# The down product of a mixture-of-experts layer: one full-precision product, or three products of rounded and remaining parts

## The reference, cut to what matters

```python
def hier_moe(h, p):
    ...
    hg = jnp.einsum('nd,edf->nef', x, p['moe_w_gate'])
    hu = jnp.einsum('nd,edf->nef', x, p['moe_w_up'])
    act = jax.nn.silu(hg) * hu * combine.astype(x.dtype)[..., None]
    y = jnp.einsum('nef,efd->nd', act, p['moe_w_down'])
    return y.reshape(b, t, d)
```

## Time and profile before

| | |
|---|---|
| median of 3 runs | 1420.52 us (1415.59 to 1420.88) |
| profiled execution: its own time as listed, the span from first to last instruction | 1411.4 us |
| TensorE busy | 1236.9 us, 88% of the span |
| VectorE busy | 678.2 us, 48% |
| ScalarE busy | 491.7 us, 35% |
| read from HBM | 295.61 MB, 211 GB/s over the span |

### The profile page before, as it was taken

How to read it: one execution, slowest core, us unless ns; L and a number is a source line. 1 busy time by engine, 2 the same in 40 slices (tenths; PEclk the granted TensorE clock), 3 DMA queues, 4 the chain that set the end, 5 groups by cost and what they waited for, 6 DMA issues and landing times.

```text
span 1411.4 us, 18228 instructions
## 1 busy us (share of the span) xinstructions
PE 1236.9 (88%) x7508; PEld 968.0 (69%) x7508; DVE 678.2 (48%) x857; ACT 491.7 (35%) x550; POOL 86.5 (6%) x93
## 2 busy tenths in 40 slices
PE   4689678998679999999967996798886999999997
PEld 3489568797656666666664985687776666666665
DVE  0255535443355556656423654445424556566652
ACT  2234521112244444444213444111322544444440
POOL 0000203130000000000000011222100000000000
PEclk8799879999789999999988997899996999999999
DMA  9744600121508888888865354102060488888960
GB/s 389 337 179 179 242 9 31 35 90 44 225 0 336 338 338 339 346 345 336 343 269 244 146 199 172 34 31 94 1 243 26 179 345 335 335 340 344 354 268 32
DMA packets 15195, 299.00 MB, mean 212 GB/s; under 512 B 1920, under 2 KB 1920, under 8 KB 2176
## 3 DMA queue, kind: packets, MB, share of 16 engines
q1 hardware_dynamic: 14688, 296.67, 53.5%
q0 software_dynamic: 416, 1.05, 0.2%
HBM read 295.61 MB, written 2.10 MB: 211 GB/s over the span
## 4 chain that ended last, share of the span: by engine, by line
PE 79%; DVE 6%; issue 5%; ACT 5%; DMA 3%; POOL 1%; SPq 0%; DVEq 0%; POOLq 0%; ACTq 0%
PE ps L824 16%; PE ps L795 8%; PE ps L796 8%; PE ps L797 8%; PE ps L713 4%; PE ps L483 3%; PE ps L485 3%; PE ps L484 3%; PE ps L663 3%; PE ps L638 3%; PE ps L659 3%; DMA param<-in_param 3%; PE ps L459 2%; PE ps L838 1%; PE ps L862 1%
## 5 line engine op out<-in xcount | busy, mean ns | idle before, releaser
L1602 DVE TENSOR_TENSOR ring_r<-ring,arena_r 128x2048 fp32r<-128x2048 f32 x124 | 284.3, 2292 | 129.5 <-ACT arena_r L1127 129.5
L1127 ACT ACTIVATE arena_r<-ring 128x2048 fp32r<-128x2048 f32 x124 | 236.7, 1909 | 231.2 <-PE ps L797 231.2
L795 PE MATMUL ps<-arena_r 128*128 128x512 f32 x512 | 231.3, 452 | 5.4 <-DVE ring_r L1602 3.5
L824 PE MATMUL ps<-ring,arena 128*128 128x512 f32 x512 | 230.3, 592 | 1.0 <-DVE arena L1608 1.0
L797 PE MATMUL ps<-ring_r,arena_r 128*128 128x512 f32 x512 | 202.5, 395 | 0.0
L796 PE MATMUL ps<-arena_r 128*128 128x512 f32 x512 | 202.3, 395 | 0.0
L824 PEld LDWEIGHTS ps<-ring,arena 128*128 128x128 f32 x512 | 96.8, 189 | 99.0 <-issue 91.9
L795 PEld LDWEIGHTS ps<-arena_r 128*128 128x128 f32 x512 | 96.3, 188 | 38.9 <-issue 16.7
L483 PE MATMUL ps<-arena_r 128*128 128x256 f32 x384 | 109.7, 286 | 10.4 <-DVE ring_r L1256 10.4
L796 PEld LDWEIGHTS ps<-arena_r 128*128 128x128 f32 x512 | 96.6, 189 | 31.8 <-issue 14.4
L797 PEld LDWEIGHTS ps<-ring_r,arena_r 128*128 128x128 f32 x512 | 96.0, 188 | 22.6
(11 more groups left out here) (301 smaller groups left out, 1548.9 us busy)
## 6 DMA issues: line engine op xcount, KB each, us to landing
ring<-in_moe SPq DMA_DIRECT2D x64, 3072.0 KB, 10.1
ring<-in_ada_w SPq DMA_DIRECT2D x16, 3072.0 KB, 11.1
ring<-in_w_feat SPq DMA_DIRECT2D x8, 3072.0 KB, 14.1
ring<-in_w_tok SPq DMA_DIRECT2D x2, 2112.0 KB, 24.0
ring<-in_w_out SPq DMA_DIRECT2D x2, 2048.0 KB, 7.3
ring<-in_w_out SPq DMA_DIRECT2D x4, 1024.0 KB, 4.9
param<-in_param SPq DMA_DIRECT2D x2, 1501.5 KB, 23.4
const<-in_const SPq DMA_DIRECT2D x1, 1899.0 KB, 16.6
```

The source lines that it names most:

```text
L795: mm(out, x_hi, hi[:, k], start=k == 0, stop=False)
L824: done = mm(bank(4 + half), act_t[:, i % 2, kk * P:(kk + 1) * P], ring[i % RING][:, at:at + 512], start=i == 0 and kk == 0, stop=i == PER_ ...
L1127: go(w_hi[:, 0:4096].rearrange("p (w n) -> p w n", w=2)[:, :, cols], ring[j][:, 0:4096].rearrange("p (w n) -> p w n", w=2)[:, :, cols], AC ...
L1602: tt(low_w, raw_w, high_w, ALU.subtract).then_inc(sem[name], 1)
```

## The change

The down product is computed like gate and up. ScalarE rounds the down weights of one expert into `down_hi` (one buffer, in a part of `param` that is free by then; 2048 columns), VectorE subtracts that from the ring slot in place. The transposed activations are rounded by ScalarE into `act_h` instead of being copied by VectorE, and VectorE subtracts to get `act_l`. TensorE makes twelve fp32r products in place of four full-precision ones. ScalarE's rounding of the down weights of e + 1 waits for the down product of e, as there is one `down_hi`. Some semaphores get the names that the other branch uses, and increments that kept unused ones in step fall away. The diff, cut to its core:

```diff
 # buffers
-        g_silu, gat, act_t = (halves(arena[:, after_w + n * 512:after_w + (n + 1) * 512]) for n in range(3))
+        g_silu, gat = (halves(arena[:, after_w + n * 512:after_w + (n + 1) * 512]) for n in range(2))
+        act_h, act_l = (halves(arena_r[:, at:at + 512]) for at in (after_w + 1024, 8192))
+        down_hi = param_r[:, PARAM["ck"].start:PARAM["ck"].start + 2048]
...
 # TensorE
                     if i >= 0:
-                        pe.wait_ge(sem["act_t"], rise(l, "act_t", e + 1))
+                        pe.wait_ge(sem["act_lo"], rise(l, "act_lo", e + 1))
+                        pe.wait_ge(sem["lo_down"], rise(l, "lo_down", e + 1))
                         if i == 0:
                             pe.wait_ge(sem["yg_lo"], rise(l, "yg_lo", turn + 1))
                         for half in range(2):
                             for kk in range(2):
-                                at = 4096 + kk * D_MODEL + half * 512
-                                done = mm(bank(4 + half), act_t[:, i % 2, kk * P:(kk + 1) * P], ring[i % RING][:, at:at + 512],
-                                          start=i == 0 and kk == 0, stop=i == PER_GROUP - 1 and kk == 1, skip_group_check=True)
+                                at = kk * D_MODEL + half * 512
+                                hi, lo = down_hi[:, at:at + 512], ring_r[i % RING][:, 4096 + at:4096 + at + 512]
+                                x_hi, x_lo = (x[:, i % 2, kk * P:(kk + 1) * P] for x in (act_h, act_l))
+                                mm(bank(4 + half), x_hi, hi, start=i == 0 and kk == 0, stop=False, skip_group_check=True)
+                                mm(bank(4 + half), x_lo, hi, start=False, stop=False, skip_group_check=True)
+                                done = mm(bank(4 + half), x_hi, lo, start=False, stop=i == PER_GROUP - 1 and kk == 1, skip_group_check=True)
                         done.then_inc(sem["down_mm"], 1)
...
 # ScalarE
+                def high_down(e, j):
+
+                    go(down_hi, ring[j][:, 4096:SLOT], ACT.Copy).then_inc(sem["hi_down"], 1)
+
                 def gathered_step(e, i, turn, ahead=2):
 
+                    if i >= 0:
+                        act.wait_ge(sem["tr_mm"], rise(l, "tr_mm", e + 1))
+                        go(act_h[:, i % 2], bank(2 + i % 2, FF), ACT.Copy).then_inc(sem["act_hi"], 1)
                     if ahead > 1:
-                        high_half(e + 2, (i + 2) % RING, "hi_a", "half_mm", 0)
+                        high_half(e + 2, (i + 2) % RING, "hi_a", "gate_mm", 0)
...
                     if ahead > 1:
-                        high_half(e + 2, (i + 2) % RING, "hi_b", "gu_mm", 1)
+                        high_half(e + 2, (i + 2) % RING, "hi_b", "up_mm", 1)
+                    if ahead > 0:
+                        if i >= 0:
+                            act.wait_ge(sem["down_mm"], rise(l, "down_mm", e + 1))
+                        high_down(e + 1, (i + 1) % RING)
...
 # VectorE
                     if i >= 0:
-                        dve.wait_ge(sem["tr_mm"], rise(l, "tr_mm", e + 1))
-                        copy(act_t[:, i % 2], bank(2 + i % 2, FF)).then_inc(sem["act_t"], 1)
+                        dve.wait_ge(sem["act_hi"], rise(l, "act_hi", e + 1))
+                        tt(act_l[:, i % 2], bank(2 + i % 2, FF), act_h[:, i % 2], ALU.subtract).then_inc(sem["act_lo"], 1)
...
                     if ahead > 1:
                         low_half(e + 2, (i + 2) % RING, "lo_b", "hi_b", 1)
+                    if ahead > 0:
+                        dve.wait_ge(sem["hi_down"], rise(l, "hi_down", e + 2))
+                        j = (i + 1) % RING
+                        tt(ring_r[j][:, 4096:SLOT], ring[j][:, 4096:SLOT], down_hi, ALU.subtract).then_inc(sem["lo_down"], 1)
```

More of the change, by code:

```diff
@@ L140 @@
     ht_hi=4, ht_lo=4, sel=1, ga_mm=8, ga_hi=8, ga_lo=8, cg_mm=1, cg_dve=1, st_mm=2, st_act=2,
-    half_mm=32, gu_mm=32, tr_mm=32, hi_a=31, hi_b=31, lo_a=31, lo_b=31, g_silu=32, g_act=32, act_t=32, yg_hi=4, yg_lo=5,
+    tr_mm=32, hi_a=31, hi_b=31, lo_a=31, lo_b=31, yg_hi=4, yg_lo=5,
     scatter_mm=4,
@@ L797, in gate_up @@
                         last = mm(out, x_hi, lo[:, k], start=False, stop=k == KT - 1)
-                    last.then_inc(sem["half_mm" if first_half else "gu_mm"], 1)
+                    last.then_inc(sem["gate_mm" if first_half else "up_mm"], 1)
                 def gathered_step(e, i, turn, last=False):
@@ L808, in gathered_step @@
                     if i >= 0:
-                        pe.wait_ge(sem["g_act"], rise(l, "g_act", e + 1))
+                        pe.wait_ge(sem["prod"], rise(l, "prod", e + 1))
                         for kk in range(2):
@@ L865, in _ @@
                             last.then_inc(sem["scatter_mm"], 1)
-                    for name, n in (("cb_mm", 16), ("gate_mm", 32), ("up_mm", 32)):
-                        pe.sem_inc(sem[name], n)
+                    pe.sem_inc(sem["cb_mm"], 16)
                 with pe.Else():
@@ L897, in _ @@
                         step(e, e % RING, last=e == N_EXPERTS - 1)
-                    for name in ("ga_mm", "cg_mm", "st_mm", "half_mm", "gu_mm", "tr_mm", "scatter_mm"):
+                    for name in ("ga_mm", "cg_mm", "st_mm", "tr_mm", "scatter_mm"):
                         pe.sem_inc(sem[name], PER[name])
@@ L1128, in high_half @@
                        ring[j][:, 0:4096].rearrange("p (w n) -> p w n", w=2)[:, :, cols], ACT.Copy).then_inc(sem[name], 1)
+                def high_down(e, j):
+                    go(down_hi, ring[j][:, 4096:SLOT], ACT.Copy).then_inc(sem["hi_down"], 1)
                 def gathered_step(e, i, turn, ahead=2):
+                    if i >= 0:
+                        act.wait_ge(sem["tr_mm"], rise(l, "tr_mm", e + 1))
+                        go(act_h[:, i % 2], bank(2 + i % 2, FF), ACT.Copy).then_inc(sem["act_hi"], 1)
                     if ahead > 1:
[L1133 removed]
+                        high_half(e + 2, (i + 2) % RING, "hi_a", "gate_mm", 0)
                     if ahead > 0:
[L1135 to L1136 removed]
+                        act.wait_ge(sem["up_mm"], rise(l, "up_mm", e + 2))
+                        go(g_silu[:, (i + 1) % 2], bank((i + 1) % 2, FF), ACT.Silu).then_inc(sem["silu"], 1)
                     if ahead > 1:
[L1138 removed]
+                        high_half(e + 2, (i + 2) % RING, "hi_b", "up_mm", 1)
[3 more added lines that the diff above has]
+                        high_down(e + 1, (i + 1) % RING)
                     if i == PER_GROUP - 1:
@@ L1161, in _ @@
                         gathered_step(N_EXPERTS - PER_GROUP + i, i, N_GROUPS - 1, ahead=PER_GROUP - 1 - i)
-                    for name, n in (("cb_act", 8), ("h_hi", 1), ("silu", 32), ("hi_gate", 31), ("hi_up", 31), ("hi_down", 32), ("act_hi", 32)):
+                    for name, n in (("cb_act", 8), ("h_hi", 1), ("hi_gate", 31), ("hi_up", 31)):
                         act.sem_inc(sem[name], n)
@@ L1178, in _ @@
                         step(e, e % RING, ahead=N_EXPERTS - 1 - e)
-                    for name in ("ga_hi", "st_act", "hi_a", "hi_b", "g_silu", "yg_hi"):
+                    for name in ("ga_hi", "st_act", "hi_a", "hi_b", "yg_hi"):
                         act.sem_inc(sem[name], PER[name])
@@ L1611, in gathered_step @@
                     if ahead > 0:
-                        dve.wait_ge(sem["g_silu"], rise(l, "g_silu", e + 2))
+                        dve.wait_ge(sem["silu"], rise(l, "silu", e + 2))
                         b = (i + 1) % 2
-                        stt(gat[:, b], ps[:, b, FF:2 * FF], cg[:, bass.ds(e + 1, 1)], g_silu[:, b], ALU.mult, ALU.mult).then_inc(sem["g_act"], 1)
+                        stt(gat[:, b], ps[:, b, FF:2 * FF], cg[:, bass.ds(e + 1, 1)], g_silu[:, b], ALU.mult, ALU.mult).then_inc(sem["prod"], 1)
                     if ahead > 1:
                         low_half(e + 2, (i + 2) % RING, "lo_b", "hi_b", 1)
+                    if ahead > 0:
+                        dve.wait_ge(sem["hi_down"], rise(l, "hi_down", e + 2))
+                        j = (i + 1) % RING
+                        tt(ring_r[j][:, 4096:SLOT], ring[j][:, 4096:SLOT], down_hi, ALU.subtract).then_inc(sem["lo_down"], 1)
                     if i == PER_GROUP - 1:
@@ L1650, in _ @@
                         gathered_step(N_EXPERTS - PER_GROUP + i, i, N_GROUPS - 1, ahead=PER_GROUP - 1 - i)
-                    for name, n in (("cb_dve", 8), ("h_lo", 1), ("lo_gate", 31), ("lo_up", 31), ("lo_down", 32), ("prod", 32),
-                                    ("act_dve", 32), ("act_lo", 32)):
+                    for name, n in (("cb_dve", 8), ("h_lo", 1), ("lo_gate", 31), ("lo_up", 31), ("act_dve", 32)):
                         dve.sem_inc(sem[name], n)
@@ L1675, in _ @@
                     residual(40, range(KT)).then_inc(sem["layer_done"], 1)
-                    for name in ("sel", "ht_lo", "ga_lo", "cg_dve", "lo_a", "lo_b", "g_act", "act_t", "yg_lo"):
```

(1 more changed line is left out.)

## The result

The changed kernel takes 1385.11 us (median of 4 runs, 1379.17 to 1390.89) where the kernel before takes 1419.64 (4 runs, 1415.59 to 1420.88): a ratio of 0.9763, 95% interval 0.9731 to 0.9795. Run again later beside other kernels it took 1391.37 against 1418.84, a ratio of 0.9816 (0.9782 to 0.9849). It is faster; 1394 was forecast.

A forecast was written before the change was run, and what follows sets the result against it. TensorE, busy for all 9.24 us of a period, was taken to bound the expert loop. The terms -40.5 + 1.9 + 8.0 + 4.2 = -26.4 us take 1420.5 to 1394 us, range 1383 to 1412.

The forecast's parts named there:

- TensorE bounds the loop: Expert loop: TensorE is busy for all 9.24 us of a period, so time taken from it shortens the kernel.
- a product costs its spacing: Down product: twelve fp32r products at 0.233 us from start to start, 2.80 us replacing 3.43, -40.5 us in all.
- The queue order: Regular expert step: the ScalarE and VectorE hand-offs arrive in time, 0.9 us to spare, so nothing stalls.
- Group ends: A group's last expert: L1619 delays the activations' low part some 0.3 us, three places in each layer, +1.9 us.
- Ends of the layers: Last expert of each layer: no next gate/up hides the hand-offs; +8.0 us of waiting and +4.2 of lower clock.
- the clock: Layer ends: after the idle stretch products start 0.43 us apart, not 0.233; 2.1 us per layer, +4.2 (0 to 4.7).
- The loads: Expert loop: 3072 KB weight loads at 365 GB/s land 2 us before they are read, so no cost.
- The bound of 433 GB/s: Weight loads: upper bound on their rate, the most shown at the kernel's start, taken over 354 from slices with expert loads.
- 64 regular steps: Expert loop: each expert gains 0.63 us, the period going from 9.24 to 8.62 us, -40.5 us.
- gaps: Before each layer's last down product: hand-offs take 4.91 us where it was 0.90, 4.0 per layer, +8.0 us.
- the rival of a cheaper end: Layer ends: they cost less than thought, by clock or order, bringing the time down to 1385; chance 7%.
- the wide range: Whole time: 1383 to 1412 us, holding forecast, transfers, cheaper end and the mild VectorE rival's near side.

The follow-up runs named there:

- the fourth product: Changed kernel plus a product of the two remaining parts, 16 fp32r products per expert in place of 12: 1447.05 us, ratio 1.0202.
- the old product and all the new work: Full-precision down products as before, with all work and waits the change gave ScalarE and VectorE: 1432.26 us, ratio 1.0095.
- Own buffer: Changed kernel, with a separate buffer for the last expert's rounded down weights, made earlier: 1380.74 us, ratio 0.9722; again 1381.23, ratio 0.9742.
- filled gap: Changed kernel plus five unused full-precision products ahead of each layer's last down product, keeping TensorE busy: 1380.39 us, ratio 0.9751.
- two products: Changed kernel without the products of remaining activations with rounded weights, 8 fp32r products per expert in place of 12: 1359.06 us, ratio 0.9559.

## Why the prediction was right

- **TensorE bounds the loop, and a product costs its spacing.** The step takes 8.60 us where 8.62 was worked out, the down product 2.80 as forecast, and the fourth product priced one at 0.236 against 0.233. The Trainium skill, TensorE: Matmul & The Clock Gate, section "Part 3: Packing small matmuls — row/col tiling", says in its list of what overlaps that a weight load overlaps with running products only where the row groups differ; the fourth product does not bear that out, since load and product together cost 0.236 us.
- **The queue order holds.** With the old product and all the new work a regular step stayed at 9.24 us. The forecast left 0.9 us ahead of the down product; 1.0 is there.
- **Group ends**: 0.26 to 0.33 us late, 0.3 forecast.
- **Ends of the layers**: a gap of 4.8 us, 4.9 forecast; the clock 2.3 us in the first layer and 1.6 in the second, 2.1 forecast for each. Own buffer and filled gap each took their part away.
- **The loads** were forecast to cost nothing, with 2 us to spare. They land after 10.8 us now, and ScalarE waits for them eight times in both layers, 3.6 us in all; the steps that take longer than they should (8.59 us, or 8.85 to 8.92 at a group's end) add up to some 0.4 us in the first profile and 1.7 in the second. One slow load in the second layer is in the chain of waits:

```profile
1207.38 12.37 DMA ring<-in_moe
1219.88 1.92 ACT arena_r L1132
```

  At 3.146 MB per 8.60 us the loads did not bind; with two products they held up single steps. The bound of 433 GB/s that the forecast leaned on came from a window of 10 us and was too high: in the four windows of 50 us between 430 and 630 us of the run with two products the loads come to 385 to 391. The Trainium skill, DMA: Bandwidth & Descriptors, section "Where 436 GB/s comes from", puts the limit at some 358 GB/s per core, as 716 GB/s of a stack shared by two cores; this kernel runs on one core, and the 388 of that run is above it.
- **The sum**: the two loops became 13.6 and 13.9 us shorter, 27.5, where -26.4 was forecast. It comes out term by term: 64 regular steps from 9.24 to 8.59 us, -41.4 before rounding (-40.5 forecast); group ends +1.7 (+1.9); gaps +7.8 (+8.0); clock +3.9 (+4.2); longer steps, put down to loads, +0.4 (nothing).
- **The number is less sure than the mechanism.** The medians moved by 34.5 us in the first comparison and by 27.5 in the second. 1385.11 lies under the 1387 to 1402 that the forecast had for itself; by its number it would belong to the rival of a cheaper end, "down to 1385", but the ends cost what was forecast. 1391.37 lies inside. Of the 34.5 us the profiled loops show 27.5; the rest is not shown in any edited stage, and the four executions of the changed kernel alone lie 11.7 us apart. That the first number fell within the wide range is in part luck.
- **A misreading in the sum**: the 9.1 us between the span of 1411.4 and the median were read as if they lay outside the span. In every execution with both numbers some 1.7 lie there (1383.62 us for a span of 1381.9). So the profiled execution of the kernel before was most likely a quick one, set against the median of others. It does not touch the forecast of 1394, which is that median less 26.4.

## What to carry to other kernels

Price a matmul by the distance from start to start in a full stream, not by its duration in the rows: 0.233 against 0.395 us decided here between a gain and a loss. When work is moved to idle engines, lay out their queues in order over one period, and then lay out the last step apart, where no next step hides the hand-offs: here some 12 of 40 us went back there (twice 3.9 us of gap, and 2.3 and 1.6 of clock), and one more buffer for the last expert took most of it out of the loops again. Before the next cut on TensorE, look at what comes right behind it: here the way through VectorE at 7.9 us, against 8.60 now, and loads that then hold up single steps. And look at the steps one by one: a mean over a loop hides a long first step, a short last one and the few that wait.

## What the runs showed of the hardware

One core drew 388 GB/s from HBM in loads of 3072 KB with the DMA engines busy for 0.98 of the time. A stage whose code is the same in all kernels took 324.4 to 332.1 us, along with the clock that TensorE was granted in it (0.92 to 0.90): more than half a per cent of the whole time, and not much less than the 10 us that the own buffer moves. So such an edit is read in its own stage first.
